# The kept cache rows of a decoder step: copied from SyncE's queue at the end of each half group, or from ScalarE's queue along the way

## The reference, cut to what matters

```
for g, (window, dil) in enumerate(GROUPS):              # (128, 1), (512, 4), (2048, 16)
    q, k, v = qkv[:, :, g, 0], qkv[:, :, g, 1], qkv[:, :, g, 2]
    buf = kv_bufs[g]                                    # the samples' cache: keys and values
    k_ctx = jnp.concatenate([buf[:, :, 0], k], axis=1)
    v_ctx = jnp.concatenate([buf[:, :, 1], v], axis=1)
    keep = min(window, p0 + T)
    new_kv.append(jnp.stack([k_ctx[:, -keep:], v_ctx[:, -keep:]], axis=2))   # an output
    o, lse = dilated_group_attn(q, k_ctx, v_ctx, ...)
```

## Time and profile before

| | us |
|---|---|
| median of three runs | 1235.96 |
| the profiled execution, its own time | 1232.21 |
| its span, first to last instruction | 1230.4 |
| TensorE busy | 1124.4 (91%) |
| ScalarE busy | 402.5 (33%) |
| TensorE's mean granted clock | 0.963 |

### The profile page before, as it was taken

One profiled execution on the slowest core, in us unless ns is written; L12 is line 12 of the kernel. 1 busy time (PEld: TensorE's weight loads), 2 busy tenths in 40 slices (PEclk: granted clock), 3 DMA queues, 4 the chain that ended last, 5 costly groups with the idle time before them and its releaser, 6 DMA issues.

```text
span 1230.4 us, 27724 instructions
## 1 busy us (share of the span) xinstructions
PE 1124.4 (91%) x11628; PEld 1004.6 (82%) x11628; DVE 503.3 (41%) x1447; ACT 402.5 (33%) x689; POOL 420.1 (34%) x205
## 2 busy tenths in 40 slices
PE   7999995599699999999999999999999999967996
PEld 7999973498598998998888899888899788855656
DVE  5999996845603106034112331410603411272324
ACT  4554445422524324224223232322422422321122
POOL 3899981533633231322222132132122122222200
PEclk9999996599799999999999999999999999989998
DMA  9988789688999799779789979887977978887662
GB/s 329 382 321 310 265 280 333 240 322 317 318 389 372 265 380 371 262 257 369 278 299 341 319 243 329 295 294 258 373 264 258 364 293 285 335 317 290 251 247 94
DMA packets 68065, 372.51 MB, mean 303 GB/s; under 512 B 12528, under 2 KB 14960, under 8 KB 65264
## 3 DMA queue, kind: packets, MB, share of 16 engines
q1 hardware_dynamic: 67952, 370.87, 83.8%
HBM read 353.22 MB, written 192.21 MB: 443 GB/s over the span
## 4 chain that ended last, share of the span: by engine, by line
PE 68%; DVE 19%; DMA 5%; issue 5%; ACT 2%; SPq 0%; POOL 0%; DVEq 0%; ACTq 0%
PE pairA L466 12%; PE pairA L467 12%; PE pairB L466 11%; PE pairB L467 11%; DVE pairD L1218 4%; DMA ring<-k_tiles 4%; PE pairC L588 4%; DVE pairC L1218 3%; DVE res L1238 2%; PE pairB L783 2%; PE pairA L783 2%; PE pairD L541 2%; PE pairC L541 2%; DVE res L1250 1%; PE pairC L594 1%
## 5 line engine op out<-in xcount | busy, mean ns | idle before, releaser
L1102 POOL TENSOR_TENSOR w_lo<-landing,w_hi 128x1024 fp32r<-128x1024 f32 x120 | 290.1, 2417 | 663.8 <-ACT w_hi L862 663.8
L862 ACT ACTIVATE w_hi<-landing 128x1024 fp32r<-128x1024 f32 x120 | 127.2, 1060 | 178.9 <-PE pairB L467 68.1
L466 PE MATMUL pairA<-act_hi,w_hi 128*128 128x288 f32 x416 | 127.8, 307 | 22.9 <-POOL act_lo L1102 11.5
L466 PE MATMUL pairB<-act_hi,w_hi 128*128 128x288 f32 x416 | 126.3, 304 | 2.9 <-DVE u_in L1198 1.2
L467 PE MATMUL pairA<-act_hi,w_lo 128*128 128x288 f32 x416 | 124.3, 299 | 0.0
L467 PE MATMUL pairA<-act_lo,w_hi 128*128 128x288 f32 x416 | 124.2, 299 | 0.0
L467 PE MATMUL pairA<-act_hi,w_hi 128*128 128x288 f32 x416 | 124.1, 298 | 0.0
L467 PE MATMUL pairB<-act_hi,w_lo 128*128 128x288 f32 x416 | 123.4, 297 | 0.0
L466 PE MATMUL pairA<-act_hi,w_lo 128*128 128x288 f32 x416 | 123.4, 297 | 0.0
L466 PE MATMUL pairA<-act_lo,w_hi 128*128 128x288 f32 x416 | 123.3, 296 | 0.0
L467 PE MATMUL pairB<-act_hi,w_hi 128*128 128x288 f32 x416 | 123.3, 296 | 0.0
(11 more groups left out here) (305 smaller groups left out, 2339.3 us busy)
## 6 DMA issues: line engine op xcount, KB each, us to landing
kept<-cache SPq DMA_DIRECT2D x64, 2040.0 KB, 16.1
landing<-w_units SPq DMA_DIRECT2D x120, 512.0 KB, 6.6
ring<-k_tiles SPq DMA_DIRECT2D x104, 512.0 KB, 5.9
ring<-v_tiles SPq DMA_DIRECT2D x104, 512.0 KB, 5.4
kept<-cache SPq DMA_DIRECT2D x16, 2016.0 KB, 19.9
kept<-cache SPq DMA_DIRECT2D x8, 960.0 KB, 13.7
kv_new<-kT SPq DMA_DIRECT2D x24, 288.0 KB, 2.5
kv_new<-vT SPq DMA_DIRECT2D x24, 288.0 KB, 9.0
```

The source lines that it names most:

```text
L466: pe.matmul(tok(at, 0, SPLIT), lhs, x[:, k, 0:SPLIT], start=first, stop=last)
L862: act.activation(w_hi[:, m % 2, :], landing[:, m % LAND, :], ACT.Copy).then_inc(hi_done, 1)
L1102: return pool.tensor_tensor(dst, src, hi.bitcast(F32), ALU.subtract)
```

## The change

The five copies of each half are taken out of SyncE's program for the later groups (the first group keeps them) and given to ScalarE, which issues them in its own DMA queue: one behind the weight split of each second unit, 1, 3, 5, 7 and 9. The same bytes are copied in the same 30 transfers. The source and destination are written with rows of `D` = 1024 floats (4 KB) in place of 16 or 32 runs.

```
-                    if i == U_CH - 1:
+                    if first and i == U_CH - 1:
                         copy_rows(0, hg * 2 + ch, 0)
                         copy_rows(1, hg * 2 + ch, 1)
                     if first and i >= 2:
                         copy_rows(2, i - 2, 4 + ch)
-                    if not first and i == U_CH - 1:
-                        copy_rows(2, (hg - 1) * 2 + ch, 2)
-                    if not first and i >= U_CH - 2:
-                        copy_rows(2, hg * 2 + ch, 6 + i - (U_CH - 2))
...
+            def copy_rows(g, b, piece):
+
+                n = COPY_ROWS[g] * 2 * D
+                src = d[f"cache{g}"][bass.ds(b, 1), (piece * n + NQ * 2 * D):(piece * n + NQ * 2 * D + n)]
+                dst = o[f"kept{g}"][bass.ds(b, 1), piece * n:piece * n + n]
+                act.dma_start(dst.rearrange("a (r m) -> (a r) m", m=D), src.rearrange("a (r m) -> (a r) m", m=D))\
+                    .then_inc(copied, 16)
+
+            def copies(hg, ch, i):
+
+                if i == 1:
+                    copy_rows(1, hg * 2 + ch, 1)
+                elif i == 3:
+                    copy_rows(2, (hg - 1) * 2 + ch, 2)
+                elif i == 5:
+                    copy_rows(2, hg * 2 + ch, 6)
+                elif i == 7:
+                    copy_rows(0, hg * 2 + ch, 0)
+                elif i == 9:
+                    copy_rows(2, hg * 2 + ch, 7)
...
                         split_hi(N_IN1, hg, U_HG, m + 2)
+                        if not first:
+                            copies(hg, ch, i)
```

## The result

The changed kernel takes **1339.36 us** (median of 4 runs, 1332.34 to 1351.54) beside 1236.52 for the kernel before: ratio 1.0843, interval 1.0754 to 1.0932. The forecast was 1260 us, its range ended at 1288. Slower was right, the size was not.

What follows compares the result with a forecast made beforehand. TensorE, busy for 91% of the span, was taken as the bound, with time falling only where it waits for transfers. 1232.2 - 10.9 gained + 39 of stalled tile loads gave 1260 us, range 1224 to 1288.

Steps and rivals of the forecast that it cites:

- The gain, 10.9 us: Without SyncE's bunch of copies, 4.1 us of later-group tile waits and 6.8 us of tail-start stops go, at most.
- ScalarE's issues, 0 us: ScalarE's 30 added copy issues cost 0 us, covered by its existing waits; uncovered they would cost 18 us.
- Rival 2: ScalarE is held by its own issues: 19 us, so 1240 us, or 1279 with slower loads too; chance 0.07.
- the copy goes first: Tile loads beside copies of units 1, 5, 7 wait for nearly the whole copy: 18.8 us a group, 56 us in all.
- I take the middle, 39 us: Stall on tile loads beside the copies, set between bounds of 22 and 56 us for three groups.
- The upper bound: Copies pass ahead of the tile loads beside them: 56 us of stalls over three groups, 1277 us in total.
- The lower bound: Copy and tile loads share bytes equally, a burst's first tile ahead: 22 us over three groups, 1243 us in total.
- The clock: TensorE's granted clock falling with stalls, outside the sum: it only stretched the slower case from 1277 up to 1290 us.
- Units 3 and 9 at 0 us: Unit 3's copy meets two tile loads with time to spare, unit 9's meets none: 0 us for both.
- 1: Tile loads hold their pace beside the copies, so the kernel gets faster: 1221 us, or 1219; chance 0.17.
- 4: Gains and stalls cancel at 11 us of stall, leaving 1232 us; chance 0.06 with similar cases.
- 3: The 4 KB pieces are not in the built program; if they were, 22 us of stalls, 1243 us; no separate chance.

Runs made afterwards that it cites:

- e3: The changed kernel with the later groups' 30 copies left out, their output rows unwritten; 1223.3 us, 0.989 of the kernel before.
- e14: The kernel before with the later groups' copies issued in SyncE's queue at the times ScalarE issued them in the changed kernel; 1331.2 us, ratio 1.079.
- e11: The changed kernel with unneeded identity products on TensorE filling its tile waits behind units 2, 6 and 8; 1319.3 us, 1.067 of the kernel before.
- e5: The changed kernel with only the copies behind units 3 and 9, the other 18 left out; 1240.3 us, 1.003 of the kernel before.
- e4: The changed kernel with its copies really cut into 4 KB pieces, same queue and places; 1304.9 us, 1.053 of the kernel before.
- e12: The changed kernel with each copy one unit earlier on ScalarE and in 16 KB pieces; 1270.6 us, 1.027 of the kernel before.
- e13: The kernel before with copies in SyncE's queue at the times ScalarE issued them when moved one unit earlier; 1280.6 us, ratio 1.036.
- e2: The changed kernel with all five copies of a half in ScalarE's queue behind unit 9's weight split; 1270.9 us, 1.028 of the kernel before.
- e10: The changed kernel with each copy one unit earlier on ScalarE (units 0, 2, 4, 6, 8), 64 KB pieces; 1271.6 us, 1.030 of the kernel before.

## Why the prediction missed: its steps one by one

1. **The gain, 10.9 us: right in size.** e3 has 12.5 us by the medians, 10.0 between the profiled executions. It isn't made up as I said, and that the sum comes out is in part luck: 6.5 us of e3's gain are idle time and 3.5 us busy time. Of the tail's 4.33 + 2.46 us the first is gone, and 2.17 us in the changed kernel, 1.86 in e3, are left at the next tile: I had named the tail's own ring loads and then counted them anyway.
2. **ScalarE's issues, 0 us: right.** 0.52 to 0.64 us each; its wait ahead of the next softmax step is 2.05 us, as in the earlier trace rows. Rival 2 named the wrong engine: it was SyncE whose issues were held, and e14 shows that these cost nothing more. (The 5.2 us of the earlier trace rows are a long issue; that the queue was full there, as I wrote, no row shows.)
3. **Which bursts: right, to the burst.** TensorE's waits for tiles counted by the unit that the burst stands behind, three groups together (this count adds up to 0.2 us more than the list above):

| behind unit | 2 | 6 | 8 | second half's 2 | 6 | 8 | others | sum |
|---|---|---|---|---|---|---|---|---|
| "the copy goes first", x 3 | 15.6 | 12.9 | 6.9 | 8.1 | 8.1 | 4.8 | 0 | 56.4 |
| measured | 15.3 | 12.8 | 9.4 | 11.1 | 11.6 | 9.2 | 2.7 | 72.1 |

4. **"I take the middle, 39 us": wrong, the first failed step.** The upper bound held behind units 2 and 6 of the first half and was too low elsewhere. In the second half I may have taken the margins too large; behind unit 8 that can't be all, since a burst waits 3.1 us there, more than the whole 2.8 us that I had for its copy. My reason for less, that a stall gives later loads time, is not borne out by the burst behind unit 6, which waits as long as the bound says although unit 2's had waited before it. What I had wrong is the order. I had the copy issued behind the split, at 503.86, and the loads entering together with it; it goes out ahead of the split, and 1.4 to 1.5 us ahead of the tile loads at all 18 tight places. So the copy was first, as in the upper bound, and in e14 one queue in order does the same. The lower bound fails too: with pieces of 4 KB, where it should have held, the waits are 48.6 us and not 22. It let a burst's first tile go ahead of the copy; the copy goes ahead of all three.
5. **The clock: the second failed step, 45 us missing from the sum.** I had it only as a tail of the range "up to 1290", from one stall in the earlier trace rows. The 72 us of waits brought 45 more, and e11 gives the 45 back.
6. **Units 3 and 9 at 0 us: wrong,** 17 us for both (e5), of it 12 busy. In the second half unit 3's copy stands ahead of the last tile of the burst behind unit 4. In the changed kernel that burst waits for 2 us in all, so the 17 us are not a further term of the sum.

By these the sum is 1232.2 - 10.9 + 72 + 45 = 1338 us, the profiled execution took 1340.5.

Of the rivals, 1 and 4 didn't happen; 3 was right that the pieces of 4 KB don't exist, and wrong on what they would give (1243; e4 has 1305). Of what I had said would show it, most did: waits in the bursts behind units 2, 6 and 8, landings of 9.5 us for copies, packets of 64 KB and no 4.33 us stall. But the waits went past the 55 us I had allowed, and the medians of the tile loads rose by only 1.1 and 1.5 us, not 2 to 5: a median over 104 loads hides the 18 bursts that pay.

On the Trainium skill, page "DMA: Bandwidth & Descriptors": section "Queues, rings and completion order" has engines take turns by whole packets, which I gave as the first bound, 1277 us. The loads beside a 64 KB copy do land behind it (the copy above at 513.5, the first tile at 515.3), and smaller pieces do less harm at these moments (1301 to 1305 us), so it agrees; a unit earlier they do no less (e12). The copy was issued ahead of the loads, and e14 shows that one queue in order does the same at these moments, so the changed kernel alone proves no rule of turns. Section "Issuing engines are not separate DMA queues", by which a second issuing engine saves issue time alone, agrees in what counts: e13 and e14 differ from their ScalarE twins by 8 to 9 us of 1300, in both directions.

**Open.** What holds SyncE's issue is not shown, only that it goes with 64 KB pieces in the other queue, and not with all of those (e2 has none). Why smaller pieces save 35 us in the changed kernel and nothing a unit earlier (e12) is not settled, and small pieces in SyncE's own queue at these moments were not run.

## What to carry to other kernels

When a transfer moves to another engine's queue, ask first at what moment that engine can issue it, and what the old queue sends just then; with pieces of 64 KB the queue itself was worth no more than 9 us here, in either direction, the moment some 70 to 80 us. Look at when the issue really goes out: here it did not wait for the work ahead of it in the program. Where a large transfer is ahead of tight loads, price those loads at the whole transfer, not at half. And price every wait of TensorE with the clock that follows it: in the changed kernel each microsecond of waiting cost another 0.6 of busy time. That is no fixed rate: e4 has 49 us of tile waits and 34 us more busy time than the kernel before, e10 34 us of waits and 8.

## What I had not expected of the hardware

- In the changed kernel, behind each of the 24 copies of units 1, 3, 5 and 7 in ScalarE's queue (q10, pieces of 64 KB), one issue of SyncE lasts 3.5 to 7 us instead of 0.3 to 0.5. With pieces of 16 KB none lasts over 2 us, and the same copies in SyncE's own queue hold nothing (1.52 us for three). It is not so behind every such copy: e10 has it behind some, and e2, with five in a bunch, behind none.
- ScalarE issues a copy before the activation ahead of it in the program has begun: 0.51 to 0.57 us before, for all 30.
- Products that nobody needs, put into the waits, made the kernel 20 us faster (1339.4 to 1319.3), since the granted clock went from 0.93 to 0.99 in the later groups.
